# A hybrid decoder layer on eight cores: u-projection jobs issued inside the first RMSNorm pass, and 1/sqrt computed as a power on GpSimd

## The reference, cut to what matters

```
h    = rmsnorm(x, g_norm1) * (1 + scale1) + shift1       # scale, shift: from a conditioning vector
proj = h @ w_in + b_in            # [u | v | glu a | glu b | gate A | gate B], 1024 columns each
u, v = gelu(u), layernorm(gelu(v))
a    = (u * chunk_mix(v)) @ w_pa + b_pa
bb   = silu(layernorm(causal_conv(ga * sigmoid(gb)))) @ w_pb + b_pb
x    = x + gate1 * ((sigmoid(gA) * a + sigmoid(gB) * bb) @ w_o)
h2   = rmsnorm(x, g_norm2) * (1 + scale2) + shift2
x    = x + gate2 * ((silu(h2 @ Wg) * (h2 @ Wu)) @ w_ffn_out)      # d_model 1024, d_ff 2816
y    = rmsnorm(x, g_final)
```

## Time and profile before

| | us |
|---|---|
| median of 2 runs (lowest, highest) | 1719.97 (1618.08, 1821.85) |
| profiled execution | 1618.01 |
| its span, slowest core (fastest core) | 1616.4 (1606.6) |
| TensorE busy / weight loads | 1428.6 / 781.9 |
| VectorE / ScalarE / GpSimd busy | 689.5 / 430.9 / 59.2 |
| ScalarE: table loads | 44, 56.5 in all |
| chain that ended last | TensorE 77%, VectorE 8%, ScalarE 4%, DMA 4% |

### The profile page before, as it was taken

The page is one execution under the profiler, slowest core; times in us unless marked ns, Lnnn a source line. Parts: engine busy times, 40 slices in busy tenths (PEclk is TensorE's granted clock), DMA queues, the critical chain, the costliest instruction groups (busy, mean ns, idle before and its releaser), DMA issues.

```text
span 1616.4 us, 22222 instructions; the slowest of 8 cores (1606.6 to 1616.4 us)
## 1 busy us (share of the span) xinstructions
PE 1428.6 (88%) x8523; PEld 781.9 (48%) x8640; DVE 689.5 (43%) x1041; ACT 430.9 (27%) x729; POOL 59.2 (4%) x76
## 2 busy tenths in 40 slices
PE   0348998999999799999998788889999997999994
PEld 0333334444544445444444554445555885444684
DVE  0463665330240152167665796862222555112234
ACT  1453665004104102311111861401111503111103
POOL 1000000000000000000000110000000000000000
PEclk9967999559999899999999899999999999999997
DMA  9882000930303405000000007344433549554662
GB/s 187 185 160 41 1 0 27 148 66 21 53 1 53 77 1 105 1 1 1 1 1 1 1 6 139 117 108 57 71 53 44 70 58 185 89 69 62 73 73 104
DMA packets 72968, 101.46 MB, mean 63 GB/s; under 512 B 1980, under 2 KB 49596, under 8 KB 72833
## 3 DMA queue, kind: packets, MB, share of 16 engines
q0 software_dynamic: 63248, 66.07, 29.5%
q1 hardware_dynamic: 9617, 33.97, 6.5%
HBM read 155.48 MB, written 12.05 MB: 104 GB/s over the span
## 4 chain that ended last, share of the span: by engine, by line
PE 77%; DVE 8%; issue 5%; DMA 4%; ACT 4%; another core or an unknown queue 1%; DVEq 0%; POOL 0%; ACTq 0%; SPq 0%; POOLq 0%
PE ps L297 74%; PE ps L300 3%; DVE ps L313 2%; DMA ADA<-w_ada 2%; ACT sqj L310 1%; DVE ps L322 1%; DVE st L816 1%; DMA A<-w_s 1%; DMA W<-w_ffn_out 1%; DVE X L313 1%; DMA CA<-cache 1%; DVE h2T L313 1%; DVE NF L319 1%; ACT L310 0%
## 5 line engine op out<-in xcount | busy, mean ns | idle before, releaser
L297 PE MATMUL ps<-h2T,W 128*128 128x512 bf16 (+1 forms) x1724 | 324.4, 348 | 10.6 <-DVE X L313 6.9
L297 PE MATMUL ps<-hT,W 128*128 128x512 bf16 (+1 forms) x1567 | 299.4, 350 | 6.8 <-ACT U L310 4.4
L297 PEld LDWEIGHTS ps<-h2T,W 128*128 128x128 bf16 x1760 | 157.5, 98 | 177.6 <-issue 13.4
L297 PEld LDWEIGHTS ps<-hT,W 128*128 128x128 bf16 x1600 | 143.3, 98 | 163.4 <-issue 17.9
L297 PE MATMUL ps<-GP,DG 128*128 128x512 bf16 x844 | 186.4, 379 | 1.1
L313 DVE TENSOR_TENSOR ACTB<-ps,SG 128x512 bf16<-128x512 f32 (+1 forms) x110 | 67.2, 612 | 250.6 <-PE ps L297 242.3
L297 PE MATMUL ps<-W,ACTB 128*128 128x256 bf16 x1496 | 165.3, 273 | 2.9 <-DVE X L313 1.7
L297 PEld LDWEIGHTS ps<-W,ACTB 128*128 128x128 bf16 x1496 | 145.9, 98 | 20.9 <-issue 3.9
L322 DVE SCALAR_TENSOR_TENSOR ps<-GP,vecT,ps 128x512 f32<-128x512 bf16 x128 | 96.6, 754 | 95.8 <-PE ps L297 85.8
L297 PEld LDWEIGHTS ps<-GP,DG 128*128 128x128 bf16 x864 | 83.5, 97 | 101.2
L310 ACT ACTIVATE U<-ps,vecT 128x512 bf16<-128x512 f32 (+1 forms) x120 | 71.6, 621 | 218.6 <-PE ps L297 218.4
(11 more groups left out here) (120 smaller groups left out, 1211.4 us busy)
## 6 DMA issues: line engine op xcount, KB each, us to landing
W<-w_ffn_in POOLq DMA_DIRECT2D x20, 1024.0 KB, 15.5
xin<-xc SPq DMA_DIRECT2D x34, 512.0 KB, 5.2
ADA<-w_ada POOLq DMA_DIRECT2D x6, 2048.0 KB, 29.6
W<-w_in POOLq DMA_DIRECT2D x6, 2048.0 KB, 22.5
W<-w_ffn_out POOLq DMA_DIRECT2D x8, 1408.0 KB, 14.6
y<-X SPq DMA_DIRECT2D x17, 512.0 KB, 3.1
W<-w_pa POOLq DMA_DIRECT2D x1, 2048.0 KB, 52.2
W<-w_pb POOLq DMA_DIRECT2D x1, 2048.0 KB, 27.2
```

Source lines behind the costliest of these rows:

```text
L297: R.op("pe", lambda e: e.matmul(out, lhsT=lhsT, rhs=rhs, start=start, stop=stop), reads=reads, writes=writes)
```

## The change

1. `rstd_from`, used by the first norm pass, v, second norm and final norm (17 tiles each), becomes the two operations that `ln_stages` has.
2. The u columns are loaded in the opening, ahead of the v columns.
3. `XIN` has seven buffers instead of eight and moves to region B; so U (region C) can be written during the pass.
4. The u jobs run token group by token group. From step 5 of the pass, up to three are issued at the end of each step, once the tiles of their group are modulated: 3, 3, 2 in steps 5 to 7, 9 to 11 and 13 to 15, and 3, 3 in steps 17 and 18: 30 jobs. The other ten are interleaved evenly with v.

```diff
+    slot_u, wv_u = wload(wi3[:, :, 0:1024], KC, 1024)
     slot_v, wv_v = wload(wi3[:, :, 1024:2048], KC, 1024)
...
     def rstd_from(col, src_ap, src_keys, scale):
-        act(rstd[:, col:col + 1], src_ap, AF.Sqrt, ..., bias=epsT[:, 0:1], scale=scale)
-        R.op("dve", lambda e: e.reciprocal(out=rstd[:, col:col + 1], in_=rstd[:, col:col + 1]), ...)
+        ts_("dve", veps2[:, col:col + 1], src_ap, float(scale), EPS, ALU.mult, ALU.add, list(src_keys), [("veps2", col)])
+        tt_("pool", rstd[:, col:col + 1], veps2[:, col:col + 1], negh, ALU.pow, [("veps2", col), ("negh",)], [("rstd", col)])
...
-    NXIN = 8
-    XIN = [M.at(f"xin{i}", [128, D], F32, OFF_C + i * 4096) for i in range(NXIN)]
+    NXIN = 7
+    XIN = [M.at(f"xin{i}", [128, D], F32, OFF_B + i * 4096) for i in range(NXIN)]
...
-    drain(skewed(n1, post=(1, pre_x2)))
-    R.fence("C")
-    slot_u, wv_u = wload(wi3[:, :, 0:1024], KC, 1024, extra_reads=[("A", 2)])
+    def gen_u_stmajor():
+        for st_ in ST512:
+            for _ in proj_fm_gen(slot_u, wv_u, KC, hT, hkey, 8, evac_u, sts=[st_]):
+                yield
+    n1g = skewed(n1, post=(1, pre_x2))
+    ug_ = gen_u_stmajor()
+    ujobs_done = 0
+    for step in range(NTT + 2):
+        next(n1g, None)
+        ndone = step - 2 + 1
+        avail = sum(8 for (t0, w) in ST512 if ndone * 128 >= t0 + w)
+        for _ in range(3):
+            if ujobs_done < avail:
+                next(ug_)
+                ujobs_done += 1
+    R.fence("B")
...
-    interleave(gen_v(), NTT + 2, proj_fm_gen(slot_u, wv_u, KC, hT, hkey, 8, evac_u), 28)
+    interleave(gen_v(), NTT + 2, ug_, 40 - ujobs_done)
```

More of the change, by code:

```diff
@@ L260, in build @@
     negh = M.at("negh", [128, 1], F32, o); o += 32
+    veps2 = M.at("veps2", [128, 64], F32, o); o += 256
     o = (o + 255) // 256 * 256
@@ L464, in rstd_from @@
     def rstd_from(col, src_ap, src_keys, scale):
-        act(rstd[:, col:col + 1], src_ap, AF.Sqrt, list(src_keys) + [("epsT",)], [("rstd", col)], bias=epsT[:, 0:1], scale=scale)
-        R.op("dve", lambda e: e.reciprocal(out=rstd[:, col:col + 1], in_=rstd[:, col:col + 1]), reads=[("rstd", col)], writes=[("rstd", col)])
+        ts_("dve", veps2[:, col:col + 1], src_ap, float(scale), EPS, ALU.mult, ALU.add, list(src_keys), [("veps2", col)])
+        tt_("pool", rstd[:, col:col + 1], veps2[:, col:col + 1], negh, ALU.pow, [("veps2", col), ("negh",)], [("rstd", col)])
     def rmsnorm_stages(src, src_keys, xn, kxn, sqj, pr, tt, dst_tile, dst_keys, mg, msh):
@@ L543, in build @@
         s = tt % NXIN
-        n1.append(rmsnorm_stages(XIN[s], [("C", "xin", s)], XN[tt % 2], ("S", "xn", tt % 2), SQJ, 2 + tt % 2, tt,
+        n1.append(rmsnorm_stages(XIN[s], [("B", "xin", s)], XN[tt % 2], ("S", "xn", tt % 2), SQJ, 2 + tt % 2, tt,
                                  hT[:, :, tt * 128:(tt + 1) * 128], [("A", tt)], M_G1, M_SH1))
@@ L548, in pre_x @@
         s = tt % NXIN
-        dma("sp", XIN[s], xc[tt * 128:(tt + 1) * 128, :], [], [("C", "xin", s)], ("xin", s))
+        dma("sp", XIN[s], xc[tt * 128:(tt + 1) * 128, :], [], [("B", "xin", s)], ("xin", s))
     for tt in range(NXIN):
@@ L555, in pre_x2, with evac_u @@
             pre_x(tt + NXIN)
-    drain(skewed(n1, post=(1, pre_x2)))
-    R.fence("C")
-    slot_u, wv_u = wload(wi3[:, :, 0:1024], KC, 1024, extra_reads=[("A", 2)])
+    def evac_u(j, t0, w, pb, bk):
+        act(U[:, j, t0:t0 + w], pb, AF.Gelu_apprx_tanh, [bk, ("vecT",)], [("C", j, tt) for tt in tts(t0, w)],
+            bias=vecT[:, j, R_BIN + 0:R_BIN + 1])
+    def gen_u_stmajor():
[14 more added lines that the diff above has]
+    R.fence("B")
     ada_load(2, extra_reads=[("A", 13)])
@@ L633, in gen_v @@
         return skewed([v_stages(tt) for tt in range(NTT)])
-    def evac_u(j, t0, w, pb, bk):
-        act(U[:, j, t0:t0 + w], pb, AF.Gelu_apprx_tanh, [bk, ("vecT",)], [("C", j, tt) for tt in tts(t0, w)],
-            bias=vecT[:, j, R_BIN + 0:R_BIN + 1])
-    interleave(gen_v(), NTT + 2, proj_fm_gen(slot_u, wv_u, KC, hT, hkey, 8, evac_u), 28)
+    interleave(gen_v(), NTT + 2, ug_, 40 - ujobs_done)
     dump("n", nB, [128, NTT, D], [("B", tt) for tt in range(NTT)])
```

## The result

The changed kernel is **slower**: median 1700.0 us (11 runs) against 1618.72 us (10 runs) of the kernel before on the same chip, a ratio of 1.0498, 95% interval [1.0486, 1.051]. Comparisons leave out disturbed, longer runs such as the 1821.85 shown at the start, so the median of 1719.97 is not used; on the chip of e5 to e8 runs of the kernel before at 1630 to 1635 us stay in beside its lowest of 1616.16, which makes the ratios of e6 and e8 about 0.8% too low, and there the lowest runs are compared as well.

A forecast was written before the change was run, and what follows sets the result against it. TensorE was taken as the pace nearly everywhere except the first norm pass. Terms 59 + 9 - 52 - 1 + 15 + 2 + 27.5 + 1.3 = +61 on 1618.0 gave 1679 us, range 1636 to 1710.

The forecast's parts named there:

- turns on ScalarE in the pass: Norm pass: the next Square waits behind the step's gelus, TensorE idles 3.3 us per three-job step; pass +59 us before restarts.
- held loads in the FFN: FFN: weight loads stand behind powers in GpSimd's queue; +15 us for q=1, +2 for q=2, +27.5 for group 1's first load.
- q=2 to the first buffer freed in group 1: FFN: q=2 load behind tile 7's power, +2 us; group 1's first load behind nine final_tile powers, +27.5.
- Rival (a): FFN: loads are not held behind powers, their price falls from 44.5 to about 3 us, total 1638; chance 0.08.
- the v stage's -52: v and u stage: 98 us against 150.1, from 13 until VectorE is fed, 83 for turns and tail 2.
- the 16 turns: v stage: VectorE becomes the bound and paces 16 v tiles at 5.2 us each, 83 us.
- the tail of 2: End of the v stage: 2 us counted after the last VectorE-paced tile.
- one in two: Norm pass: TensorE restarts at the low clock in half of nine steps, about 2 us each, +9 us.
- Rival (c): Norm pass: TensorE at low clock throughout, +47 us instead of +9, total 1717; chance 0.08.
- Rival (b): Norm pass: the turn on ScalarE costs nothing, pass +33 us instead of +59 and no restarts, total 1644; chance 0.13.
- Rival (d): Norm pass: Square is not in gelu's table set, extra table loads cost +12 us, total 1691; chance 0.06.
- Rival (e): Norm pass: u lands late or x starves, jobs slip and nothing overlaps, total 1690 to 1710; chance 0.03.

The follow-up runs named there:

- e5: Changed kernel with v tiles taking their two PSUM banks strictly in turn; ratio 1.0495 to the kernel before, lowest run 1698.52 us.
- e8: Changed kernel with the edits of e4, e5, e6 and e7 together; ratio 0.9776 to the kernel before, lowest run 1592.22 us.
- e6: Changed kernel with w_s loaded and prepared in the opening and b_s before the v stage; ratio 1.029 to the kernel before, lowest run 1676.05 us.
- e1: Kernel before with the power on GpSimd in all four norms, no u job moved; ratio 1.0227, profiled span 1655.8 us.
- e3: Changed kernel with w_ffn_out loads and group 1's first load issued one block earlier, ahead of the powers; median 1660.1 us, ratio 1.0253 to the kernel before.
- e7: Changed kernel with Sqrt back in the FFN norm and final_tile, the power kept in pass and v; lowest run 1650.37 us.
- e2: Changed kernel with Sqrt and reciprocal back in all four norms, u jobs still in the pass; median 1719.4 us, ratio 1.063 to the kernel before.
- e4: Changed kernel with a pass step's gelus issued behind the next step's Square and Identity; ratio 1.0242 to the kernel before, lowest run 1657.44 us.
- e9: e8 without the overlap, all 40 u jobs after the pass beside v; median 1587.97 us, ratio 0.981 to the kernel before.

## Why the prediction was right and wrong

The sign and the two main mechanisms were right: slower, from turns on ScalarE in the pass and held loads in the FFN. The size was +61 and the trace shows +83 between profiled spans. Nearly all of the missing 22 us lie on one side: 9 in the v stage, 5.5 at the start of the mixing, 5 in the pass, 4 in the opening and the gap. Taken between the same events:

| stage | predicted | measured |
|---|---|---|
| opening | 0 | +2.2 |
| pass, with restarts | +68 | +72.8 |
| gap behind it | 0 | +1.9 |
| v stage | -52 | -43.1 |
| start of the mixing | (not in the sum) | +5.5 |
| up to the FFN out projection | -1 | -0.5 |
| q=1 of group 0 | +15 | +13.0 |
| q=2 to the first buffer freed in group 1 | +29.5 | +29.6 |
| end | +1.3 | +1.9 |

**The FFN and the end** came out as worked: +44.5 for +45.8. The q=1 load went out at 1322.29 on the heels of the fifth power, TensorE waited 10.2 us for it (13.2 predicted); the first load of group 1 followed the ninth power of `final_tile`. That TensorE waited 30.3 us there and not the 20 of the forecast does not change the sum: `final_tile` took 4.51 us a tile instead of 4.16 (+0.35, predicted +0.32), and nothing of group 1 ran beside it any more. The earlier trace rows was the one row that told this, a load on the heels of a power, and it held in every run that had the powers there. Rival (a) is dead by e1, e3 and e7.

**The step that failed is the v stage's -52, in its first term: 13 us until VectorE is fed.** The stage took 107.0 us and not 98, and the head was 20.8 us and not 13, from the first v matmul (207.62) to the first finished tile:

```profile
216.27 1.02 ACT L311 ACTIVATE vr<-ps 128x1024 f32<-128x1024 f32 x1 [21.41 <-PE ps L298]
...
223.85 1.29 DVE L634 BATCH_NORM_STATS2 st<-vr 128x6 f32<-128x512 f32 x2 [4.60 <-ACT vr L311]
...
228.39 1.22 DVE L314 TENSOR_TENSOR nB<-vr,ps 128x1024 bf16<-128x1024 f32 x1 [0.58 <-DVE vr L314]
```

Two things were left out. The code is skewed: tile 0 is scaled only behind the statistics of tile 1, so VectorE idles from its first statistics to 223.85 and needs 4.5 us more for a first result; the 16 turns of the sum do not contain this one. And TensorE feeds it 3 us later than I had it: a v tile is 20 matmuls, 16 of `w_in` and four of the bias, not the 18 of my sum, and takes 4.7 us at the high clock and not 3.9 (8.5 at the low), and a u job stands between the first two. I had costed a stage that starts full; before, TensorE set the pace and u jobs filled its queue through this head.

The other two terms were right in sum, 86.2 us from the first finished tile to the third conditioning block (314.63) against 85, by luck in part: the 16 turns took 5.4 us each and not 5.2 (see e5), and the tail of 2 was not there. "VectorE becomes the bound" was half true for the same reason.

The same fault, cover counted as if it stayed, gives **the missing +5.5**: the load of `b_s` (318.80, 5 us to its landing) is wanted at once, and before the change it went out at 272.80, 8 us ahead of the end of the last u jobs, which hid it. And it gives the miss of e2. The u jobs had filled the start, the turns and the end of the v stage, and the change took most of them away.

**The pass** was near, +72.8 for +68. The gap of 3.3 us was 3.1. The size that was off is the restart. I took one in two; the nine steps with jobs took 97.8 us between Identities against 82.8 without any restart, so about +15, not +9: the transposes behind the nine gaps took 1.20 to 1.94 us against 1.07, and the jobs behind them 0.25 to 0.30 a matmul. Rival (c), low clock throughout, asked for +47 and did not come. Rival (b), that the turn costs nothing, is what e4 makes true by hand: it is worth 40 us, and the prediction's 35 for turn and restarts was low by 5.

**Rival (d)** is dead: Square ran under gelu's table without a load, 4 loads in the whole kernel. **Rival (e)** had the right time (1690 to 1710) for a reason that did not come: `u`'s weights landed 68.4 us after their issue at 4.4, and the first job ran at 79.26 (near 76 predicted), so the overlap took place.

The opening and the gap, +4.1 together, are within what the profiles differ by (first Identity 61.2 to 65.0 with `w_s` behind the pass; last transposes to first v matmul 25.3 to 28.2 in before, after, e1, e2, e3, e4 and e7).

**Open**: what the power is worth alone in e9 was not run. e1's v stage is 6.1 us shorter than before; e9's is 149.3, but it starts with the `LVGs` copies that stood in the gap before. Also the source of e6's earlier opening is argued and not shown: with `w_s` first, the x loads leave at 13.9 instead of 6.7 us, and TensorE's longest wait for `w_ada` falls from 23.4 to 10.2.

## What to carry to other kernels

A queue that carries both small operations and loads makes every load as late as the operation ahead of it: before putting an operation there, write down each load that follows it in program order and when it goes out today. When work moves out of a stage, ask what it covered there (the fill of a skewed pipeline, a late load, a ring of table switches), because these come up as new waits. Place the evacuation of moved work behind the instructions of the chain that sets the pace, or the overlap turns into taking turns. And price both stages after the move: the jobs filled TensorE in the one and left it waiting for VectorE in the other, and what one gained the other lost.

## What the runs showed of the hardware

**The power is slower beside VectorE's scaling.** It takes 0.55 us in the pass, even beside a TENSOR_TENSOR of VectorE that reads PSUM (88.59, 1.23 us; the power at 88.79), and in the FFN, but 1.03 us in every v tile after the first (the first has no scaling beside its power, and takes 0.57). There it starts 0.19 us after a fp32 TENSOR_SCALAR of 0.81 us (237.32) and ends 0.41 us behind its end. The Trainium skill ("SBUF — State Buffer", Who interferes with whom) says that VectorE and GpSimd share one pair of ports, that a tensor_scalar can take both, and that whoever issues first then holds the pair for its whole instruction; the trace agrees, with a power that is 0.48 us longer beside the 0.62 us of scaling that are left when it starts. It costs nothing here, being a step ahead of its use.

**Table loads cost no drain.** In e2 a gelu ends at 261.09, the load runs from 261.11 to 262.39, and Sqrt starts at 262.41; the earlier trace rows have the same. The Trainium skill ("ScalarE: Activation LUTs", What ACT_TABLE_LOAD costs) adds a drain of about 1.38 us to each switch; the trace does not agree with it.

**Gaps of 3 us, and the low clock behind them.** In the pass TensorE's granted clock is 0.84. Behind its nine gaps of 3.0 to 3.1 us eight transposes took 1.20 to 1.94 us; 1.07 is what they take at the higher of its two levels (2.4 GHz) and 1.94 at the lower (1.2). In e4, the same work with 10.3 us of waits for Identity instead of 33.8, the clock was 0.96 over the pass.
